# Result rows gathered in two rounds, and the last expert's rows selected in two parts, in a two-layer trunk with top-2 experts

## The chip, the core and the metric

The kernel is one program on 1 core of one Trainium2 chip. It is measured by device microseconds from the launch to the end of the program, median of several runs. TensorE (PE) multiplies, VectorE (DVE) and ScalarE (ACT) move and compute elementwise, GpSimd (POOL) issues the indexed transfers, SyncE (SP) issues the loads of the weights. Each engine runs its own list of instructions in order, and they meet at semaphores only.

## What is computed

A trunk of two layers over 512 tokens of width 1024, float32. Layer 0 mixes with an mLSTM and differential attention, layer 1 with a short gated convolution. Behind either mixer stands the part that the change is about: a router picks for each token one group of four experts and two experts in it, out of sixteen in all, and adds their weighted outputs.

```python
def hier_moe(h, wg, bg, we, be, w_gate, w_up, w_down):
    ...
    _, gsel = lax.top_k(glog, 1)
    ...
    top_v, top_i = lax.top_k(elog_g, EXPERT_TOP_K)
    top_w = jax.nn.softmax(top_v, axis=-1)
    eid = gsel * EXPERTS_PER_GROUP + top_i
    combine = jnp.einsum('tk,tke->te', top_w, jax.nn.one_hot(eid, N_EXPERTS, dtype=jnp.float32)) * pg[:, None]
    ...
    for e in range(N_EXPERTS):
        y = (jax.nn.silu(t @ w_gate[e]) * (t @ w_up[e])) @ w_down[e]
        out = out + combine[:, e:e + 1] * y

def reference(x, ...):
    for layer in range(DEPTH):
        h = rmsnorm(x, norm_mix[layer])
        ...
        x = x + y.astype(x.dtype)
        h = rmsnorm(x, norm_ffn[layer])
        x = x + hier_moe(h, ...).astype(x.dtype)
    return rmsnorm(x, norm_final)
```

## The kernel before

**Weights and precision.** Every large product runs as three fp32r matmuls on a high and a low part of both operands (`mm3`, L1834 to L1838). SP loads the weights into `ring`, six slots of 1 MB, two chunks each; ScalarE writes the high part of a chunk (L672, in layer 1's mixer with a gain, L670), VectorE the low part (L1073, L1070). Both parts lie in `w_split`, which holds six chunks, so ScalarE starts on a chunk when TensorE has finished the one six before it.

**Experts.** An expert has room for 96 tokens (`CAP`). GpSimd gathers the rows of the tokens of the next expert (L617), TensorE turns them (`turn_xg`, L2171). The step of expert e on TensorE is: its gate (4 chunks), the turning of the activations of expert e-1 (L2195), its up projection (4 chunks), the turning of expert e+1's rows, and the down projection of e-1 (4 chunks). In the step of expert 14 the activations of 14 itself are turned midway through the down projection of 13, so that expert 15's step can begin with the down projection of 14. VectorE's part of a step: half of an output row copied (L1633), the low parts of the weights, the low part of the activations (`copy_actT`, L1597), the gated product (`hidden`, L1604), the low part of the next rows (L1590). ScalarE copies the other half and issues the store of the 96 rows to `y_rows_dram` (L955).

**The way back.** `result_rows` (L1542 to L1562) computes on VectorE where in `y_rows_dram` each token's two rows lie, `back_idx`; a token whose row is of expert 15 gets the index of its other row there, since expert 15 is not fetched. When experts 0 to 14 are stored, GpSimd issues eight gathers, for four tiles of 128 tokens two each, into `y_back` (`take_back`, L634). VectorE adds them to the tokens with their weights (`combine`, L1535). The rows of expert 15 come by TensorE: a selection matrix `selT` times `y_sb` as plain fp32 (`last_rows`, L2270), added by `add_last` (L1523). Expert 15's rows are stored all the same (L950). In layer 1 the last tile is summed wholly on TensorE (L2279 to L2281). If an expert has more than 96 tokens, a branch that each engine takes on `overflow_flag` handles the rest; it is not taken here.

After layer 0's experts VectorE combines tiles 0 and 1, adds the last expert's rows, splits the first odd weights, and ScalarE squares and scales the tiles for the next norm (L716, L722), GpSimd computes the roots (L539, L542), TensorE turns them (L1811). After layer 1's experts the same leads to the final norm and the stores of the result. `keep_busy` (L1826) is filler: matmuls whose result nobody reads.

## Time and profile before

| | us |
|---|---|
| median of 3 runs | 1113.03 |
| lowest, highest | 1112.18, 1113.85 |
| span of the profiled execution | 1108.9 |

The span runs from the first to the last instruction of one execution; the difference to the median lies around it. TensorE is busy for 1078.4 us of it, VectorE for 870.7, ScalarE for 662.6, GpSimd for 114.7. A timeline row gives the start, the duration, the engine, the line and the operation; in square brackets the idle time ahead of it and what ended it. A row of the waits gives who waited for whom. "PEld" is the load of a weight into TensorE. In the chain of waits each row is released by the one above it. Windows give the busy time of the engines in a stretch.

### The profile page before, as it was taken

The numbers are of one execution on the slowest core, as the hardware profiler recorded it, in microseconds if no ns is written. First come the engines' busy times: TensorE is split into PE (matmuls) and PEld (weight loads), VectorE is DVE, ScalarE is ACT, GpSimd is POOL, SyncE is SP. The second block draws the span as 40 slices with busy tenths as digits, with TensorE's granted clock in tenths as the row PEclk, the third lists the DMA queues.
The fourth block names the chain that finished last, engine by engine and source line by source line (L and its number), as shares of the span: only waits on it lengthen the run. The fifth ranks groups of instructions, "written<-read, shape, count | busy, mean of one in ns | idle before, by whom it ended". The sixth has DMA issues, their size and how long they took to land.

```text
span 1108.9 us, 15258 instructions
## 1 busy us (share of the span) xinstructions
PE 1078.4 (97%) x5352; PEld 875.6 (79%) x5352; DVE 870.7 (79%) x1139; ACT 662.6 (60%) x848; POOL 114.7 (10%) x160
## 2 busy tenths in 40 slices
PE   7999999999999999999999999999999999999996
PEld 5777777678878888888886888878978888888883
DVE  5256765788799999999999453654699999999997
ACT  5224444523488888878876413222488888778872
POOL 2010000222120000011013000000120000010013
PEclk9999999999999999999999999999999999999998
DMA  9742222112389999999999522332189999999985
GB/s 326 196 149 77 86 86 77 62 72 77 115 304 392 406 396 397 408 393 410 399 386 327 177 79 77 114 100 90 77 305 392 406 396 396 409 395 410 400 338 211
DMA packets 78643, 285.89 MB, mean 258 GB/s; under 512 B 17687, under 2 KB 17687, under 8 KB 62204
## 3 DMA queue, kind: packets, MB, share of 16 engines
q1 hardware_dynamic: 66396, 241.64, 57.0%
q0 software_dynamic: 8464, 30.42, 8.3%
q10 hardware_dynamic: 3728, 13.11, 2.9%
q8 instruction: 33, 0.54, 0.2%
q14 instruction: 22, 0.18, 0.0%
HBM read 266.27 MB, written 20.20 MB: 258 GB/s over the span
## 4 chain that ended last, share of the span: by engine, by line
PE 67%; DMA 15%; DVE 10%; ACT 3%; issue 2%; POOL 2%; POOLq 0%; DVEq 0%; SPq 0%; ACTq 0%
PE ps L1836 20%; PE ps L1838 19%; PE ps L1837 19%; DMA ring<-in_exp_w_gate 10%; DVE w_split L1073 5%; ACT w_split L672 2%; DMA arena<-h_rows_dram,arena 2%; DMA arena<-y_rows_dram,arena 1%; PE ps L2171 1%; DMA y_rows_dram<-arena 1%; PE ps L2085 1%; POOL arena L634 1%; PE ps L2107 1%; PE ps L1811 1%; PE ps L1920 1%
## 5 line engine op out<-in xcount | busy, mean ns | idle before, releaser
L1073 DVE TENSOR_TENSOR w_split<-ring,w_split 128x1024 fp32r<-128x1024 f32 x428 | 505.1, 1218 | 46.8 <-ACT w_split L672 39.1
L672 ACT CAST w_split<-ring 128x1024 fp32r<-128x1024 f32 x428 | 441.8, 1052 | 128.6 <-PE ps L1838 90.2
L1836 PE MATMUL ps<-w_split,hT 128*128 128x512 f32 (+1 forms) x976 | 385.6, 395 | 3.7 <-DVE hT L1581 1.7
L1838 PE MATMUL ps<-w_split,hT 128*128 128x512 f32 (+1 forms) x976 | 377.7, 387 | 0.0
L1837 PE MATMUL ps<-w_split,hT 128*128 128x512 f32 (+1 forms) x976 | 376.8, 386 | 0.0
L1836 PEld LDWEIGHTS ps<-w_split,hT 128*128 128x128 f32 x976 | 183.5, 188 | 43.8 <-issue 2.9
L1838 PEld LDWEIGHTS ps<-w_split,hT 128*128 128x128 f32 x976 | 183.3, 188 | 38.0
L1837 PEld LDWEIGHTS ps<-w_split,hT 128*128 128x128 f32 x976 | 183.7, 188 | 34.1
L1836 PE MATMUL ps<-hT,w_split 128*128 128x512 f32 (+1 forms) x384 | 144.8, 377 | 1.8 <-DVE hT L1109 1.0
L1837 PE MATMUL ps<-hT,w_split 128*128 128x512 f32 (+1 forms) x384 | 142.8, 372 | 0.0
L1838 PE MATMUL ps<-hT,w_split 128*128 128x512 f32 (+1 forms) x384 | 142.8, 372 | 0.0
L1836 PEld LDWEIGHTS ps<-hT,w_split 128*128 128x128 f32 x384 | 72.3, 188 | 20.5 <-issue 6.9
L617 POOL DMA_INDIRECT arena<-h_rows_dram,arena x30 | 40.1, 1337 | 413.1 <-PE ps L2171 394.0
L1838 PEld LDWEIGHTS ps<-hT,w_split 128*128 128x128 f32 x384 | 72.3, 188 | 12.8
L1837 PEld LDWEIGHTS ps<-hT,w_split 128*128 128x128 f32 x384 | 72.4, 188 | 12.1
L670 ACT ACTIVATE w_split<-ring,odd_gain 128x512 fp32r<-128x512 f32 x48 | 31.3, 715 | 46.6 <-PE ps L1838 46.4
L1070 DVE SCALAR_TENSOR_TENSOR w_split<-ring,odd_gain,w_split 128x512 fp32r<-128x512 f32 x48 | 33.0, 746 | 31.1 <-ACT w_split L670 30.8
L539 POOL TENSOR_SCALAR st<-st 128x1 f32<-128x1 f32 (+1 forms) x27 | 10.1, 374 | 342.3 <-ACT arena L716 233.6
L716 ACT ACTIVATE arena<-x_sb 128x1024 f32<-128x1024 f32 x19 | 20.1, 1061 | 38.6 <-DVE x_sb L1371 20.7
L805 ACT ACTIVATE x_sb<-x_sb,st 128x128 f32<-128x128 f32 (+3 forms) x32 | 17.8, 557 | 38.0 <-DVE st L1202 38.0
L1590 DVE TENSOR_TENSOR hT<-ps,hT 128x768 fp32r<-128x768 f32 x30 | 28.4, 948 | 3.1 <-ACT hT L893 3.1
L1197 DVE SCALAR_TENSOR_TENSOR x_sb<-ps,arena 128x256 f32<-128x256 f32 (+3 forms) x16 | 13.1, 821 | 18.9 <-PE ps L1920 18.9
(271 smaller groups left out, 914.0 us busy)
## 6 DMA issues: line engine op xcount, KB each, us to landing
ring<-in_exp_w_gate SPq DMA_DIRECT2D x64, 1024.0 KB, 12.5
ring<-in_exp_w_up SPq DMA_DIRECT2D x64, 1024.0 KB, 12.5
ring<-in_exp_w_down SPq DMA_DIRECT2D x64, 1024.0 KB, 13.2
ring<-in_w_in_even SPq DMA_DIRECT2D x14, 1024.0 KB, 11.4
y_rows_dram<-arena ACTq DMA_DIRECT2D x32, 384.0 KB, 7.0
ring<-in_w_in_odd SPq DMA_DIRECT2D x12, 1024.0 KB, 8.7
ring<-in_w_out_even SPq DMA_DIRECT2D x4, 1024.0 KB, 4.7
h_rows_dram<-arena POOLq DMA_DIRECT2D x8, 512.0 KB, 3.2
```

The costliest lines, as they stand in the source:

```text
L617: g.indirect_dma_start(out=xg[0:CAP, e % 2, :], out_offset=None, in_=h_dram, in_offset=bass.IndirectOffsetOnAxis(ap=slot_tok[0:CAP, e:e + ...
L670: ins = s.activation(hi_of(c)[:, row], raw(c)[:, row], ACT.Copy, scale=scale)
L672: ins = s.copy(hi_of(c), raw(c))
L716: s.activation(junk, x_sb[:, t, :], ACT.Square, accum_out=st[:, t:t + 1]).then_inc(sumsq_ready, 1)
L805: s.activation(e_maps[:, u % 2, m, 0:n], e_maps[:, u % 2, m, 0:n], ACT.Exp, bias=st[:, 16 + c:17 + c], accum_out=st[:, 20 + c:21 + c]).the ...
L1070: ins = v.scalar_tensor_tensor(out=lo_of(c)[:, row], in0=raw(c)[:, row], scalar=scale, in1=hi_of(c)[:, row].bitcast(F32), op0=ALU.mult, op ...
L1073: ins = v.tensor_tensor(lo_of(c), raw(c), hi_of(c).bitcast(F32), ALU.subtract)
L1197: v.scalar_tensor_tensor(out=e_maps[:, u % 2, :, 0:n], in0=src, scalar=64.0 ** -0.5, in1=bc(bias_sb[:, h % 2, T - n:T], 1, P, 2, n), op0=A ...
L1590: v.tensor_tensor(xgT[:, u, 1, :, 0:CAP], ps[:, 5:7, :].rearrange("p b (k c) -> p (b k) c", k=4)[:, :, 0:CAP], xgT[:, u, 0, :, 0:CAP].bitc ...
L1836: mm(out, a[0], b[0], start=start, stop=False)
L1837: mm(out, a[1], b[0], start=False, stop=False)
L1838: return mm(out, a[0], b[1], start=False, stop=stop)
```

## The change

**Two rounds of gathers.** Behind the last gather of tokens GpSimd issues eight gathers that read only the rows of experts 0 to 11 (`EARLY`, 1152 rows): `bounds_check` lets them skip an index beyond. They wait until experts 0 to 11 are stored, until `result_rows` is done and until `sel_last` is turned (its memory is part of `y_back`). When expert 14 is stored and the first round has landed, eight more gathers follow with `late_idx`, in which the indices below 1152 have 3072 added, so that these are skipped. A tile is there when four gathers have landed instead of two.

**`result_rows` and the selection matrix earlier.** For this VectorE runs `result_rows` ahead of the step of expert 14 (before: behind it), with two operations more. TensorE turns `sel_last` ahead of that step too (before: behind the down projection of expert 14), and ScalarE copies it to `selT` there.

**The last expert.** Its output is no longer stored. ScalarE writes the high part from PSUM to `y_last` (in `hT`, where the even experts' rows were), VectorE the low part (`last_low`, two subtractions), and `last_rows` multiplies both parts by `selT` as fp32r, 16 matmuls in layer 0 and 12 in layer 1. In layer 1 ScalarE copies the fp32 rows to `y_sb` as well, for the last tile. Its tile order is 0, 2, 1, and the two matmuls that don't need gathered rows stand ahead of the wait for them. `last_rows` has two filler matmuls instead of four.

**VectorE at the ends.** Of the odd weights, the first two chunks are split ahead of the combines in layer 0. The combines of tiles 0 and 1 stand in the branches, with `last_low` between them. A semaphore is merged with another at the start.

```diff
@@ pool, experts @@
                 pool.wait_ge(xg_turned, E * (l + 1))
+                pool.wait_ge(flag_ready, l + 1)
+                pool.wait_ge(last_sel_turned, l + 1)
+                pool.wait_ge(y_stored[0], stores_before(l, E - E // GROUPS))
+                pool.wait_ge(y_stored[1], stores_before(l, E - E // GROUPS + 1))
+                for t in range(TT):
+                    for k in range(2):
+                        c = 2 * t + k
+                        g.indirect_dma_start(out=y_back[:, t, k, :], out_offset=None, in_=y_dram[0:EARLY, :],
+                                             in_offset=bass.IndirectOffsetOnAxis(ap=back_idx[:, c:c + 1], axis=0),
+                                             bounds_check=EARLY - 1, oob_is_err=False).then_inc(y_back_loaded[t], 16)
...
+                pool.wait_ge(y_stored[0], 16 * (E // 2) * (l + 1))
+                pool.wait_ge(y_stored[1], 16 * (E // 2 - 1) * (l + 1))
+                for t in range(TT):
+                    pool.wait_ge(y_back_loaded[t], 64 * l + 32)
...
                 with pool.Else():
-                    take_back((E - 1) * CAP)
+                    take_back((E - 1) * CAP, late_idx)
@@ act @@
+            def copy_y_parts(l, down_done):
+                act.wait_ge(chunk_done, down_done)
+                for half in range(2):
+                    s.copy(y_last[0:CAP, 0, half * 512:half * 512 + 512], ps[0:CAP, 2 + half, :]).then_inc(y_last_hi, 1)
+                if l:
+                    act.wait_ge(y_stored[1], stores_before(l, E - 1))
+                    for half in range(2):
+                        act.wait_ge((y_half0, y_half1)[half], E * (l + 1))
+                        s.copy(y_sb[0:CAP, 1, half * 512:half * 512 + 512], ps[0:CAP, 2 + half, :]).then_inc(y_last_hi, 1)
...
-                copy_last_y(1, 2, c + 16, 16 * (n // 2))
-                store_y(E - 1, n, 1)
+                copy_y_parts(l, c + 16)
@@ dve @@
-                v.tensor_copy(back_idx, rt[:, 592:600]).then_inc(flag_ready, 1)
+                link(v.tensor_scalar(late_f, rt[:, 592:600], float(EARLY), float(2 * E * CAP), ALU.is_lt, ALU.mult))
+                v.tensor_copy(back_idx, rt[:, 592:600])
+                v.tensor_tensor(late_idx, late_f, rt[:, 592:600], ALU.add).then_inc(flag_ready, 1)
...
                 for e in (E - 3, E - 2):
-                    step(e, n0 + e, e % 2, step_chunk(l, e), None, 16 * ((n0 + e - 2) // 2))
+                    if e == E - 2:
+                        result_rows(l)
+                    step(e, n0 + e, e % 2, step_chunk(l, e), None, stores_before(l, e - 2))
                 n, c = n0 + E - 1, step_chunk(l, E - 1)
-                result_rows(l)
...
+                if l == 0:
+                    splits(c + 18)
...
+                def last_low():
+                    for half, copied in enumerate((y_half0, y_half1)):
+                        cs = slice(half * 512, half * 512 + 512)
+                        dve.wait_ge(y_last_hi, 4 * l + half + 1 - l * 2)
+                        v.tensor_tensor(y_last[0:CAP, 1, cs], ps[0:CAP, 2 + half, :], y_last[0:CAP, 0, cs].bitcast(F32),
+                                        ALU.subtract).then_inc(copied, 1)
...
+                with dve.Else():
+                    if l:
+                        end_weights()
+                    combine(l, 0)
+                    last_low()
+                    combine(l, 1)
@@ pe, last_rows @@
-                keep_busy(4, 0)
+                keep_busy(2, 0)
...
-                for half in range(2):
-                    cs = slice(half * 512, half * 512 + 512)
+                halves = [slice(half * 512, half * 512 + 512) for half in range(2)]
+                for half, cs in enumerate(halves):
                     mm(ps[:, 6 + half, :], end_selT, y_sb[0:CAP, 1, cs], start=True, stop=False)
+                pe.wait_ge(y_back_loaded[TT - 1], 128)
```

The order of VectorE's instructions at the end of layer 0's experts, before. L1633 opens the step of expert 14, L1545 to L1562 are `result_rows`.

```order
L1633 COPY arena<-ps 96x512
L1073 TENSOR_TENSOR w_split<-ring,w_split 128x1024 x4
L1597 TENSOR_TENSOR hT<-ps,hT 128x4x96
L1073 TENSOR_TENSOR w_split<-ring,w_split 128x1024 x4
L1604 TENSOR_TENSOR arena<-arena,ps 96x512
L1590 TENSOR_TENSOR hT<-ps,hT 128x8x96
L1073 TENSOR_TENSOR w_split<-ring,w_split 128x1024 x2
L1597 TENSOR_TENSOR hT<-ps,hT 128x4x96
L1073 TENSOR_TENSOR w_split<-ring,w_split 128x1024 x2
L1545 TENSOR_SCALAR overflow_flag<-arena 128x1
L1546 SCALAR_TENSOR_TENSOR arena<-arena 128x8
```

The same place now; the lines of the split, of L1633 and of L1597 have become L1103, L1665 and L1629, and `result_rows` begins at L1575 (first fence its beginning, second its end).

```order
L1103 TENSOR_TENSOR w_split<-ring,w_split 128x1024 x4
L1575 TENSOR_SCALAR overflow_flag<-arena 128x1
L1576 SCALAR_TENSOR_TENSOR arena<-arena 128x8
L1578 TENSOR_TENSOR arena<-arena,iota_slot 128x64
L1579 TENSOR_TENSOR arena<-arena 128x128
```

```order
L1592 TENSOR_SCALAR arena<-arena 128x8
L1593 CAST arena<-arena 128x8
L1594 TENSOR_TENSOR arena<-arena 128x8
L1665 COPY arena<-ps 96x512
L1103 TENSOR_TENSOR w_split<-ring,w_split 128x1024 x4
L1629 TENSOR_TENSOR hT<-ps,hT 128x4x96
L1103 TENSOR_TENSOR w_split<-ring,w_split 128x1024 x4
```

`result_rows` stood behind the step's last two splits and now stands ahead of its first operation, with L1592 and L1594 added.

VectorE's order behind layer 0's experts before: L1624 is the last operand of expert 15, L1535 the combines, L1523 `add_last`, L1070 the split of odd weights, two instructions a chunk. The first fence is what stands ahead of the branch, the second what stands behind it.

```order
L1073 TENSOR_TENSOR w_split<-ring,w_split 128x1024
L1614 TENSOR_TENSOR arena<-arena,ps 96x256
L1073 TENSOR_TENSOR w_split<-ring,w_split 128x1024
L1624 TENSOR_TENSOR hT<-ps,hT 128x2x96
L1688 TENSOR_LOAD overflow_flag
```

```order
L1535 SCALAR_TENSOR_TENSOR x_sb<-arena,x_sb 128x1024 x4
L1523 SCALAR_TENSOR_TENSOR x_sb<-ps,arena,x_sb 128x1024 x2
L1070 SCALAR_TENSOR_TENSOR w_split<-ring,odd_gain,w_split 128x512 x2
L1523 SCALAR_TENSOR_TENSOR x_sb<-ps,arena,x_sb 128x1024 x2
L1070 SCALAR_TENSOR_TENSOR w_split<-ring,odd_gain,w_split 128x512 x2
```

And now: L1656, L1100, L1565, L1734 (`last_low`) and L1553.

```order
L1646 TENSOR_TENSOR arena<-arena,ps 96x256
L1103 TENSOR_TENSOR w_split<-ring,w_split 128x1024
L1656 TENSOR_TENSOR hT<-ps,hT 128x2x96
L1100 SCALAR_TENSOR_TENSOR w_split<-ring,odd_gain,w_split 128x512 x4
L1739 TENSOR_LOAD overflow_flag
```

```order
L1565 SCALAR_TENSOR_TENSOR x_sb<-arena,x_sb 128x1024 x2
L1734 TENSOR_TENSOR hT<-ps,hT 96x512 x2
L1565 SCALAR_TENSOR_TENSOR x_sb<-arena,x_sb 128x1024 x2
L1777 UNCONDITIONAL_BRANCH
L1553 SCALAR_TENSOR_TENSOR x_sb<-ps,arena,x_sb 128x1024 x4
```

Four instructions of odd splits moved from among the adds to ahead of everything, and two subtractions stand between the combines.

TensorE's end of layer 1, before and now (L2264 and L2318 turn the last tile's selection, L2270 and L2328 select the other tiles, L2279 and L2347 select for the last tile).

```order
L1826 MATMUL ps<-later,ones 128x512 x4
L2264 MATMUL ps<-arena 96x128
L2270 MATMUL ps<-arena,hT 128x512 x6
L2279 MATMUL ps<-arena 128x512
L2280 MATMUL ps<-arena 128x512
L2281 MATMUL ps<-arena 128x512
```

```order
L1884 MATMUL ps<-later,ones 128x512 x2
L2318 MATMUL ps<-arena 96x128
L2328 MATMUL ps<-hT 128x512 x12
L2347 MATMUL ps<-arena 128x512 x2
L2350 MATMUL ps<-arena 128x512
L2351 MATMUL ps<-arena 128x512
```

The selection matmuls are twice as many, of another type, and both that select for the last tile stand ahead of the products with the gathered rows.

## Rows read from the trace of the kernel before

**Rows 1.** The page, parts 1 and 4: busy time; the chain by engine.
```profile
PE 1078.4 (97%) x5352; PEld 875.6 (79%) x5352; DVE 870.7 (79%) x1139; ACT 662.6 (60%) x848; POOL 114.7 (10%) x160
...
PE 67%; DMA 15%; DVE 10%; ACT 3%; issue 2%; POOL 2%; POOLq 0%; DVEq 0%; SPq 0%; ACTq 0%
```

**Rows 2.** Chain of waits, layer 1's tail: start us, us, what.
```profile
1070.03 6.00 DMA y_rows_dram<-arena
...
1076.29 1.17 POOL arena L634
...
1085.45 8.55 DMA arena<-y_rows_dram,arena
...
1095.24 0.86 PE ps L2280 x2
...
1101.63 1.45 POOLq L75
```

**Rows 3.** Windows: us, then busy us per engine, granted clock, DMA share, GB/s.
```profile
544.90:563.80 18.90, 18.84 (x93) 15.27 (x91) 18.90 (x21) 15.83 (x18) 0.00 (x0) 1.00 1.02 416
1044.10:1065.10 21.00, 20.77 (x102) 16.83 (x101) 21.00 (x22) 17.80 (x21) 0.57 (x1) 1.00 1.02 415
```

**Rows 4.** Waits, layer 1 (first two), layer 0: us, times, longest.
```profile
PEld ps L1836 <- DVE hT L1597: 0.7, 1, 0.7
...
PEld ps L2195 <- DVE arena L1604: 0.2, 1, 0.2
...
PEld ps L1836 <- DVE hT L1597: 0.5, 1, 0.5
```

**Rows 5.** VectorE timeline, layer 1: start us, us, engine, line, operation.
```profile
1058.76 0.68 DVE L1604 TENSOR_TENSOR arena<-arena,ps 96x512 f32<-96x512 f32 x1
...
1062.50 0.55 DVE L1597 TENSOR_TENSOR hT<-ps,hT 128x384 fp32r<-128x384 f32 x1
...
1065.23 0.14 DVE L1545 TENSOR_SCALAR overflow_flag<-arena 128x1 int32<-128x1 f32 x1
...
1068.00 0.17 DVE L1562 CAST arena<-arena 128x8 int32<-128x8 f32 x1
1068.08 1.22 DVE L1073 TENSOR_TENSOR w_split<-ring,w_split 128x1024 fp32r<-128x1024 f32 x1
```

**Rows 6.** VectorE timeline, end of layer 0.
```profile
583.79 0.35 DVE L1624 TENSOR_TENSOR hT<-ps,hT 128x192 fp32r<-128x192 f32 x1
584.72 2.60 DVE L1535 SCALAR_TENSOR_TENSOR x_sb<-arena,x_sb 128x1024 f32<-128x1024 f32 x2 [0.58 <-DMA arena<-y_rows_dram,arena]
...
590.85 2.48 DVE L1523 SCALAR_TENSOR_TENSOR x_sb<-ps,arena,x_sb 128x1024 f32<-128x1024 f32 x2
593.24 1.41 DVE L1070 SCALAR_TENSOR_TENSOR w_split<-ring,odd_gain,w_split 128x512 fp32r<-128x512 f32 x2
```

**Rows 7.** ScalarE, then TensorE, end of layer 0.
```profile
583.42 3.79 ACT L670 ACTIVATE w_split<-ring,odd_gain 128x512 fp32r<-128x512 f32 x6
...
596.32 2.14 PE L1811 MATMUL ps<-ident,arena 128*128 128x128 f32 x16 [1.20 <-ACT arena L722]
```

**Rows 8.** VectorE (first two), then ScalarE, end of layer 1.
```profile
1084.26 5.24 DVE L1535 SCALAR_TENSOR_TENSOR x_sb<-arena,x_sb 128x1024 f32<-128x1024 f32 x4
...
1099.57 0.69 DVE L1791 TENSOR_TENSOR x_sb<-ps,x_sb 128x512 f32<-128x512 f32 x1 [1.89 <-PE ps L2281]
...
1086.56 0.58 ACT L919 COPY arena<-ps 96x512 f32<-96x512 f32 x1 [3.81 <-PE ps L1838]
```

**Rows 9.** Windows behind the last matmul, columns as in rows 3.
```profile
1099.60:1103.60 4.00, 0.00 (x0) 0.00 (x0) 3.56 (x4) 0.72 (x2) 1.78 (x2) 0.96 0.32 130
1103.60:1108.00 4.40, 0.00 (x0) 0.00 (x0) 0.92 (x2) 0.00 (x0) 0.00 (x0) 0.50 0.61 239
```

**Rows 10.** Line L634, result gathers: ns min, median, max.
```profile
L634 POOL DMA_INDIRECT arena<-y_rows_dram,arena x16: 937/986/1880, 577.5 to 1085.5; - x16
```

**Rows 11.** Line L315, weight loads of layer 1's last steps.
```profile
DMA to landing us min/median/max: 11.3/12.5/13.6
```

129 lines of the change are left out of this document (76 added, 53 removed).

## The prediction

> **What bounds the kernel now.** I read the page first, then the chain of waits, then the busy windows, then the timelines of the places that the diff touches. TensorE is busy 97% of the span and carries 67% of the chain that ended last [rows 1]: where it runs, the time is TensorE's. The diff touches four short places: the step of expert 14 and the tail after expert 15, in either layer. The question is what ends last there.
>
> At the end of layer 1 the chain of waits says: the store of expert 14's rows starts at 1070.03 and takes 6.00 us, only then GpSimd issues eight gathers, the last is issued at 1085.45 and lands 8.55 us later, and then TensorE sums the last tile [rows 2]. This is the path that the early gathers aim at. But a chain shows one path, not what runs beside it at the same length. So look at VectorE: in 1044.10 to 1065.10 it is busy 21.00 us of 21.00, and in layer 0 18.90 of 18.90; the DMA engines are full there too (415 GB/s) [rows 3]. And TensorE waits in both layers for VectorE's last operation of that stretch, L1597, which makes the activation operand of expert 14: 0.7 and 0.5 us on the weight load, and 0.2 us for L1604 [rows 4]. VectorE, without a gap, already sets TensorE's pace in that step.
>
> **1. The row numbers move ahead of step 14.** `result_rows` ran behind that step. It takes from 1065.23 to 1068.08, 2.85 us [rows 5]; TensorE then had split weights in hand and no wait follows. The change puts it ahead of L1633 of step 14, in the gapless stretch. It gains two operations and a link: the link costs about 0.2 us and the rest 0.1 (L1562 lasts 0.17 us, and the next one starts 0.08 behind it [rows 5]). Sum 3.15 us. Behind it stand 4 splits, L1597, 4 splits, L1604, L1590, 2 splits, L1597. None of them has idle time ahead of it that could swallow the delay, so the first L1604 (1058.76) and the second L1597 (1062.50) come 3.15 us later, and TensorE with them: it waits at the transposes of expert 14's activations and at the down projection. Bounds: 0, if something I don't see lets VectorE catch up; 3.5, if ScalarE, whose store waits for L1633, adds a little. I take **+3.1 us** of TensorE time per layer. Nothing comes back in the step of expert 15: the queue there is free of `result_rows`, but TensorE did not wait for it there. The four selection transposes and ScalarE's copy of them, which move to the same place, take under 0.6 us of ScalarE, which is not full; nothing.
>
> **2. End of layer 0.** VectorE's last operand stands at 584.14 (L1624), it waits 0.58 us for gathered rows, combines tiles 0 and 1 with one more wait, and starts the first `add_last` at 590.85 [rows 6]. From its end hang square, norm, scaling, the transposes at 596.32 (1.20 us of idle TensorE) and all that follows [rows 7]. After the change the same stretch holds, from 587.3 (584.14 + 3.1): two chunks of split odd weights moved ahead of the combines (1.41 us for two halves, so 2.8 [rows 6]), preceded by 0.5 us of wait for ScalarE (its six halves start at 583.42, now 586.5, and the first two end 1.3 us later [rows 7]); combine 0, 2.6 us (L1535 x2 [rows 6]); the low parts of expert 15's rows, two subtractions from PSUM like L1604, which lasts 0.68 us [rows 5], overlapped 1.2; combine 1, 2.6. 587.3 + 0.5 + 2.8 + 2.6 + 1.2 + 2.6 = 597.0, against 590.85: **+6.1 us**. The gathers are no longer awaited: expert 14's store, 3.1 later, lands at about 580.3, and a second-round pair needs some 3 us of issue and under 6 of landing, so tile 0 stands before 590.6. That removes both waits (0.58 and about 0.9), but the moved splits and the new subtractions are longer. Eight plain fp32 selection matmuls become sixteen fp32r ones; TensorE was ahead of VectorE there, so this gives nothing.
>
> **3. End of layer 1.** VectorE combined tiles 0 and 1 in 5.24 us from 1084.26 and had a wait of 1.89 us before the last half of tile 3, at 1099.57 [rows 8]. After: combine 0 ends at 1090.0 (+3.1). The low parts need ScalarE's copies, which can't start before TensorE's last matmul (L919 at 1086.56 [rows 8], now 1089.7), so they run 1090.3 to 1091.5. Then the old sequence, without its 1.89 us of wait: everything behind `add_last` 0 is 4.6 us late (3.1 + 0.3 + 1.2), less about 2.0: VectorE ends tile 3's second half 2.6 us later than before. TensorE is ready by then (1098.4 by the same bookkeeping: end_sel and low parts 1091.5, tile 1 by 1093.1, six fp32 products of 0.87 us as in [rows 2]). Behind it stand ScalarE's square of tile 2 and two halves, now back to back, up to 3.5 us late; GpSimd's last power step took 1.45 us [rows 2] beside a VectorE that was busy, and may be shorter once VectorE is done. Bounds 2.6 and 3.5; I take **+3.0 us**.
>
> **4. The clock.** The last matmul ends at 1099.57, where L1791 starts [rows 8]. TensorE's granted clock is 0.96 in the mean of the 4.0 us behind it and 0.50 after that [rows 9], 1.2 of 2.4 GHz. In layer 0 TensorE, done with the short matmuls at about 597, now waits to 602.4 for the first scaled tile, 5.4 us instead of 1.20 [rows 7]. That is longer than the gap which ended in the fall, so a fall is more likely than not. The transposes there take 2.14 us [rows 7] and would take up to 2.1 more, the nine filler matmuls behind them 1.9. Bounds 0 and 3; I take **+1.5 us**.
>
> **5. The gathers themselves.** A gather costs GpSimd 0.94 to 1.88 us [rows 10]; with the bound a skipped row may cost nothing or as much as a fetched one. Even at the old 8.55 us of landing [rows 2], tile 3 would stand at 1098 and the products at 1101.6, before VectorE asks for them at 1102.2. Nothing either way. The early round starts at about 1057.4, behind the transposes of expert 15's rows.
>
> **Sum.** 6.1 + 3.0 + 1.5 = 10.6 us on the profiled span of 1108.9. The median of the runs is 1113.03, 4.1 us above the span; I add the same difference: 1113.0 + 10.6 = **1123.6 us**. A measurement of this kernel can tell about 0.2%, 2.2 us, from no change.
>
> **Rivals.** (a) *The gather chain was the only thing that ended last.* For it: the chain itself [rows 2]. Then the 1.5 us of waits in layer 0 and the 1.9 in layer 1 go and nothing takes their place: 1113.0 - 3.4 = **1109.6**. It decides if VectorE has 3 us to spare in step 14 and 4 in the tails. Against it: [rows 3] and [rows 6]. 0.08.
> (b) *Step 14 absorbs the row numbers, the tails don't.* Layer 0 then has 6.1 - 3.1 = 3.0, layer 1 3.0 - 3.1, about 0: **1116.0**, or down to 1113.5 if ScalarE's copies come a little early. Against it the gapless stretch. 0.12, a third of it within 0.2% of before.
> (c) *The early gathers hold up the weights.* Twelve of sixteen experts' rows, 3.1 of the 4.2 MB that eight gathers of 128 rows of 4 KB move, now flow while the DMA engines are full with expert 15's weights [rows 3]: 7.6 us of transfer at 415 GB/s. A load takes 12.5 us to land [rows 11], and the split ring lies up to six chunks ahead of TensorE, so I expect most of it hidden. If half comes through, with or without slower gathers (all at 1.88 us, a second round ends 7 us later), both layers lose 2 to 4 us more: about **1129**. 0.17.
> The Trainium skill, "DMA: Bandwidth & Descriptors", section "Queues, rings and completion order", says that each DMA engine takes turns between the queues that have work. By it the weights would keep about half of the bandwidth while the gathers last, and the delay would be nearer to the small end; no run here shows two long queues beside each other. The same notes, "SBUF — State Buffer", say that GpSimd can be locked out by VectorE operations with two SBUF inputs; by that rule the early gathers, issued beside the splits, would be the slow ones. The row has 1.88 at most [rows 10], and the first round has some 20 us.
> (d) *The change does not do what it says:* the bound doesn't save a row's transfer. By part 5 that changes nothing; it belongs to the forecast.
>
> **How the numbers follow.** Forecast 0.63 (1119 to 1127 by its bounds), (a) 0.08, (b) 0.12, (c) 0.17. The predicted time is the forecast's. The range runs from (b) with a small margin to the middle of (c), 1115.5 to 1129.5; it leaves out (a), a part of (b) and the upper half of (c), about 0.2. Faster by over 0.2%: 0.08, rival (a). Within 0.2%: 0.04, of (b). Slower: the rest, 0.88.
>
> **What would show it.** In the profile of the changed kernel: a wait of TensorE for VectorE of 2 to 3 us in step 14 of either layer (right for step 1; none means (a) or (b)); the first `add_last` of layer 0 about 6 us later, with VectorE busy ahead of it and no wait for a gather (step 2); no TensorE wait at the last tile, VectorE without a gap from combine 0 to the end (step 3); a granted clock under 1.00 behind the transposes of layer 1's first norm (step 4; none, and 1.5 us go). ScalarE waiting for loads near the early gathers would be (c). A second-round gather that VectorE waits for would break part 5.

## The result and the profile after

The changed kernel takes 1126.12 us (median of 6 runs, 1122.67 to 1127.55), the kernel before in the same comparison 1112.61 us (6 runs, 1109.52 to 1114.47). The ratio is 1.0121, 95% interval 1.0104 to 1.0138: 13.5 us slower. The prediction was 1123.6 us, range 1115.5 to 1129.5, with 0.88 for slower.

The profiled run of after is 1127.55 us, its span 1125.8, against 1108.9 before: 16.9 us between the two profiles. So the profiles themselves stand 3.4 us further apart than the medians, and a difference between two spans has to be taken apart before it is explained. The page, parts 1, 3 and 4, of after:

```profile
PE 1084.0 (96%) x5348; PEld 882.5 (78%) x5348; DVE 874.1 (78%) x1147; ACT 662.2 (59%) x850; POOL 149.0 (13%) x176
...
q0 software_dynamic: 10768, 30.43, 8.3%
...
PE 77%; DVE 8%; DMA 7%; ACT 3%; issue 3%; POOL 2%; POOLq 0%; DVEq 0%; SPq 0%; ACTq 0%
```

Against [rows 1] the chain has less DMA and more TensorE: the path through expert 14's store and its gathers, which ended last before, is not the one that the chain picks now. In layer 0 it picks the early round instead: its gathers up to the one at 577.19, which lands 5.60 us later, and then the second round up to the wait of VectorE. GpSimd is 34 us busier, with 16 more operations.

**Where the time went.** The clearest measure is the length of the two stretches that the change touches, from the first VectorE operation of step 14 to a fixed mark behind the tail: the first projection matmul of the odd layer for layer 0, the last scaled row for layer 1. VectorE's timeline of after, then two rows of before for the same marks (start us, us, engine, line, operation, idle time ahead and its releaser), then TensorE's first projection of after and of before:

```profile
549.85 0.14 DVE L1575 TENSOR_SCALAR overflow_flag<-arena 128x1 int32<-128x1 f32 x1
...
552.98 0.68 DVE L1665 COPY arena<-ps 96x512 f32<-96x512 f32 x1
...
563.13 0.67 DVE L1636 TENSOR_TENSOR arena<-arena,ps 96x512 f32<-96x512 f32 x1
...
1060.15 0.14 DVE L1575 TENSOR_SCALAR overflow_flag<-arena 128x1 int32<-128x1 f32 x1
...
1118.66 1.41 DVE L1121 SCALAR_TENSOR_TENSOR arena<-x_sb,st,arena 128x512 f32<-128x512 f32 x2 [1.09 <-POOL st L569]
```
```profile
549.39 0.68 DVE L1633 COPY arena<-ps 96x512 f32<-96x512 f32 x1
...
1048.61 0.68 DVE L1633 COPY arena<-ps 96x512 f32<-96x512 f32 x1
...
1103.10 1.42 DVE L1091 SCALAR_TENSOR_TENSOR arena<-x_sb,st,arena 128x512 f32<-128x512 f32 x2 [0.44 <-POOL st L559]
```
```profile
610.19 0.36 PE L1894 MATMUL ps<-hT,w_split 128*128 128x256 f32 x1
```
```profile
600.96 0.35 PE L1836 MATMUL ps<-hT,w_split 128*128 128x256 f32 x1 [0.54 <-issue]
```

Layer 0's stretch: 600.96 - 549.39 = 51.57 us before, 610.19 - 549.85 = 60.34 after, **+8.8**. Layer 1's: 54.49 before, 58.51 after, **+4.0**. Together +12.8 of the 13.5 us. The two spans differ in three more places: 0.5 us ahead of step 14 of layer 0, 2.3 us between the two stretches, and 1.3 us behind the last scaled row. The first two lie where the two programs are alike. Between the stretches the kernels of this document take 446.3 to 452.2 us (before 447.65), and a part of that is the granted clock in layer 1's routing, which moves from run to run; windows of before (first) and after, columns as in rows 3:

```profile
790.00:800.00 10.00, 9.41 (x71) 8.99 (x71) 7.62 (x36) 5.74 (x7) 3.00 (x6) 0.83 0.53 210
800.00:811.00 11.00, 10.14 (x75) 8.98 (x75) 9.70 (x21) 7.12 (x10) 3.86 (x2) 1.00 0.27 89
```
```profile
790.00:800.00 10.00, 10.00 (x59) 8.68 (x58) 4.17 (x22) 3.21 (x4) 0.12 (x1) 0.83 0.01 2
800.00:811.00 11.00, 10.40 (x80) 9.98 (x80) 8.36 (x37) 6.03 (x7) 2.99 (x6) 0.84 0.48 191
```

The 1.3 us at the end are a part of the change; the section on the experiments comes back to them. In what follows every kernel is read by these two stretches; the median of the runs stands beside them.

**Step 14.** Waits of TensorE in after, layer 0 (first) and layer 1 (line waited for: us, times, longest), and windows of layer 0:

```profile
PE ps L2253 <- DVE arena L1636: 1.7, 1, 1.7
...
PE ps L2253 <- DVE arena L1636: 2.1, 1, 2.1
```
```profile
564.00:566.00 2.00, 2.00 (x9) 1.66 (x9) 2.00 (x3) 0.48 (x1) 1.70 (x2) 0.66 1.02 426
566.00:568.00 2.00, 2.00 (x6) 1.51 (x5) 1.51 (x3) 1.04 (x1) 1.82 (x1) 0.50 0.98 391
```

`result_rows` takes 3.13 us (549.85 to 552.98), L1636 comes 3.1 us later behind the start of the stretch, and TensorE waits for it where it did not before ([rows 4] had 0.2 us). In layer 0 the granted clock, at 1.00 up to 564, falls behind that wait to 0.50, 1.2 of 2.4 GHz, for some 3 us. VectorE's last operand of expert 15 (L1656) starts at 588.07, 38.22 us behind the start of the stretch, where [rows 6] gives 583.79 - 549.39 = 34.40: 3.8 us. Layer 1, where the clock stays at 1.00, has 37.23 against 34.40. So 2.8 us are the row numbers and 1.0 is the clock.

**Layer 0's tail.** VectorE, then GpSimd's gathers (L638 the last of the first round, L654 the second round), then TensorE, all of after:

```profile
588.07 0.35 DVE L1656 TENSOR_TENSOR hT<-ps,hT 128x192 fp32r<-128x192 f32 x1
589.08 2.74 DVE L1100 SCALAR_TENSOR_TENSOR w_split<-ring,odd_gain,w_split 128x512 fp32r<-128x512 f32 x4 [0.66 <-ACT w_split L690]
591.74 2.60 DVE L1565 SCALAR_TENSOR_TENSOR x_sb<-arena,x_sb 128x1024 f32<-128x1024 f32 x2
594.37 1.28 DVE L1734 TENSOR_TENSOR hT<-ps,hT 96x512 fp32r<-96x512 f32 x2
596.46 2.60 DVE L1565 SCALAR_TENSOR_TENSOR x_sb<-arena,x_sb 128x1024 f32<-128x1024 f32 x2 [0.80 <-DMA arena<-y_rows_dram,arena]
599.31 4.86 DVE L1553 SCALAR_TENSOR_TENSOR x_sb<-ps,arena,x_sb 128x1024 f32<-128x1024 f32 x4 [0.24 <-PE ps L2328]
```
```profile
560.17 3.95 POOL L638 DMA_INDIRECT arena<-y_rows_dram,arena  x1 [33.98 <-PE ps L2229]
...
577.19 1.80 POOL L638 DMA_INDIRECT arena<-y_rows_dram,arena  x1 [0.30 <-issue]
584.66 0.99 POOL L654 DMA_INDIRECT arena<-y_rows_dram,arena  x1 [5.66 <-issue]
```
```profile
604.11 3.68 PE L1869 MATMUL ps<-ident,arena 128*128 128x128 f32 x16 [3.33 <-ACT arena L742]
```

The first `add_last` comes 49.46 us behind the start of the stretch instead of 41.46, +8.0. VectorE is all but full on the way, yet it waits 0.80 us for a gather: the second round starts at 584.66, where the gathers of before started at 577.47 (first row of L634 in [rows 10]). Both chains, VectorE's work and the gathers, end within a microsecond of each other. This is the sentence on which the experiments hang.

From the first `add_last` to the first projection it is 10.88 us instead of 10.11. The transposes take 3.68 us at half clock where they took 2.14, but they start 4.80 us behind `add_last` instead of 5.47: GpSimd's first two small steps take 0.19 and 0.57 us here, and took 0.63 and 0.96 us before.

**Layer 1's tail.** The last rows of VectorE and two of GpSimd beside them, of after:

```profile
1101.63 1.28 DVE L1734 TENSOR_TENSOR hT<-ps,hT 96x512 fp32r<-96x512 f32 x2 [0.40 <-ACT hT L957]
...
1116.29 1.28 DVE L1121 SCALAR_TENSOR_TENSOR arena<-x_sb,st,arena 128x1024 f32<-128x1024 f32 x1 [0.72 <-POOL st L552]
```
```profile
1114.46 1.17 POOL L549 TENSOR_SCALAR st<-st 128x1 f32<-128x1 f32 x1 [1.56 <-ACT arena L736]
...
1116.34 1.28 POOL L562 TENSOR_SCALAR st<-st 128x1 f32<-128x1 f32 x1
```

There is no wait for the last tile's products any more, VectorE goes through; but its small helper steps on GpSimd, 0.2 us elsewhere, take 1.2 us beside VectorE's work and are waited for.

### The profile page after: what moved, and what is told of

Its sections match the earlier page's. It is cut to its first block, busy times and chain, and to the rows that moved or that the text cites. A ratio compares the mean times of both kernels' runs of the same rounds, so it can differ in the third digit from the quotient of the medians.

```text
span 1125.8 us, 15308 instructions
## 1 busy us (share of the span) xinstructions
PE 1084.0 (96%) x5348; PEld 882.5 (78%) x5348; DVE 874.1 (78%) x1147; ACT 662.2 (59%) x850; POOL 149.0 (13%) x176
## 3 DMA queue, kind: packets, MB, share of 16 engines
q0 software_dynamic: 10768, 30.43, 8.3%
## 4 chain that ended last, share of the span: by engine, by line
PE 77%; DVE 8%; DMA 7%; ACT 3%; issue 3%; POOL 2%; POOLq 0%; DVEq 0%; SPq 0%; ACTq 0%
PE ps L1894 23%; PE ps L1896 22%; PE ps L1895 22%; DMA ring<-in_exp_w_gate 4%; DVE w_split L1103 3%; PE ps L2229 2%; DMA arena<-h_rows_dram,arena 2%; PE ps L1869 1%; ACT w_split L692 1%; DMA arena<-y_rows_dram,arena 1%; DVE x_sb L1565 1%; PE ps L2143 1%; POOL arena L638 1%; PE ps L1978 1%; PE ps L2092 1%
## 5 line engine op out<-in xcount | busy, mean ns | idle before, releaser
L1103 DVE TENSOR_TENSOR w_split<-ring,w_split 128x1024 fp32r<-128x1024 f32 x428 | 505.1, 1219 | 52.8 <-ACT w_split L692 45.8
L1896 PEld LDWEIGHTS ps<-hT,w_split 128*128 128x128 f32 x384 | 72.4, 188 | 12.6
L1100 DVE SCALAR_TENSOR_TENSOR w_split<-ring,odd_gain,w_split 128x512 fp32r<-128x512 f32 x48 | 32.9, 746 | 31.7 <-ACT w_split L690 31.5
L638 POOL DMA_INDIRECT arena<-y_rows_dram,arena x16 | 33.2, 2072 | 73.9 <-PE ps L2229 69.6
```

The source lines that it names most:

```text
L638: g.indirect_dma_start(out=y_back[:, t, k, :], out_offset=None, in_=y_dram[0:EARLY, :], in_offset=bass.IndirectOffsetOnAxis(ap=back_idx[:, ...
L1100: ins = v.scalar_tensor_tensor(out=lo_of(c)[:, row], in0=raw(c)[:, row], scalar=scale, in1=hi_of(c)[:, row].bitcast(F32), op0=ALU.mult, op ...
L1103: ins = v.tensor_tensor(lo_of(c), raw(c), hi_of(c).bitcast(F32), ALU.subtract)
L1896: return mm(out, a[0], b[1], start=False, stop=stop)
```

## Experiments

The table gathers all of them. L0 and L1 are the two stretches described above, "sum" their sum against before's 106.06 us; the ratio is to before on the same chip.

| kernel | L0 | L1 | sum | median us | ratio, 95% |
|---|---|---|---|---|---|
| before | 51.57 | 54.49 | 0 | 1112.61 | |
| after | 60.34 | 58.51 | +12.8 | 1126.12 | 1.0121 (1.0104 to 1.0138) |
| rows_ahead | 55.35 | 57.14 | +6.4 | 1117.92 | 1.0042 (1.0026 to 1.0058) |
| rows_back | 62.51 | 64.09 | +20.5 | 1136.37 | 1.0204 (1.0188 to 1.0221) |
| odd_back | 59.63 | 59.57 | +13.1 | 1128.07 | 1.0146 (1.0129 to 1.0164) |
| fill | 58.84 | 58.50 | +11.3 | 1128.74 | 1.0147 (1.0128 to 1.0166) |
| bound1152 | 63.60 | 61.70 | +19.2 | 1132.95 | 1.0166 (1.0148 to 1.0184) |
| one_round | 59.46 | 58.46 | +11.9 | 1126.51 | 1.0105 (1.0082 to 1.0127) |
| hold_clock | 58.75 | 58.55 | +11.2 | 1125.08 | 1.0098 (1.0078 to 1.0118) |
| gps_after | 56.43 | 55.54 | +5.9 | 1121.31 | 1.0073 (1.0052 to 1.0093) |
| sel_fp32 | 61.04 | 57.64 | +12.6 | 1127.91 | 1.0140 (1.0117 to 1.0164) |
| branch_first | 58.47 | 59.53 | +11.9 | 1127.29 | 1.0140 (1.0118 to 1.0161) |
| gps_before | 52.40 | 53.61 | -0.1 | 1112.48 | 1.0003 (0.9986 to 1.0019) |
| gps_sel_one | 53.88 | 55.11 | +2.9 | 1114.74 | 1.0032 (1.0017 to 1.0047) |

Each stretch is from one profiled execution, so a microsecond between two of them is not much; the medians carry some 2 us of their own. Three things can be told apart:

- **The clock in step 14.** In nine kernels the row numbers stand ahead of step 14 on VectorE, and TensorE waits there for 1.3 to 2.1 us. Behind that wait the granted clock fell to 0.50 in layer 0 of after, rows_ahead, odd_back, one_round, hold_clock and sel_fp32, and in layer 1 of rows_ahead, odd_back and branch_first. There the last operand of expert 15 starts 38.2 to 38.3 us behind the start of the stretch, in the other nine places 37.2 to 37.3. A fall costs 1.0 us, and it came or stayed away in the same code, so two stretches are to be compared with the same number of falls.
- **The end.** Behind the last scaled row the span goes on for 5.8 to 5.9 us in the five kernels without an early round (before, rows_ahead, gps_before, one_round, gps_sel_one) and for 7.1 to 7.2 us in the nine with one. GpSimd's closing drain is what ends last there, 6.24 us in one_round and 7.54 us in after. So the early round costs 1.3 us more that no stretch holds, and the sum for the changed kernel is +14.1 us.
- **Layer 1's tail before.** From the last operand to the last scaled row it takes 20.09 us in the profile of before, and 18.86 in both rows_ahead and gps_before, which have the same code there. So 54.49 may be 1.2 us long, and the cost in layer 1 that much higher.

My theory after the result: VectorE's 3.1 us in step 14 go one to one to TensorE; in the tail VectorE is the bound, and the rest is the clock. The rivals: the tail makes up for step 14; the gathers set the end.

### 1. The row numbers alone (rows_ahead)

The kernel before with

```
                 for e in (E - 3, E - 2):
+                    if e == E - 2:
+                        result_rows(l)
...
                 n, c = n0 + E - 1, step_chunk(l, E - 1)
-                result_rows(l)
```

> The kernel before with one edit: its own row numbers (2.85 us of VectorE) ahead of step 14 in both layers. Theory: plus 2.85 us of TensorE time per layer, plus 0.7 in layer 0 if the clock falls there too: 1112.6 + 6.4 = 1119.0 us. The rival, by which step 14 absorbs them or the tail makes up for them: 1112.6; they then cost less behind the step than they did ahead of it, and the end of layer 1, where VectorE had 1.89 us of wait, could take up to 2 of it: 1117.

Measured: 1.0042, 4.7 to 5.4 us; the stretches +3.8 and +2.65, sum 6.4, the size expected but not made up as expected. The last operand of expert 15 comes 3.9 us later in both layers (38.28 against 34.40), 2.9 by the row numbers and 1.0 by the clock; layer 1's tail is 1.2 us shorter, as it is in gps_before, where nothing stands ahead of step 14. TensorE waits 2.1 us for VectorE's L1604 in either layer, and the clock falls in both; layer 0:

```profile
555.00:575.00 20.00, 17.85 (x80) 14.33 (x80) 17.39 (x18) 15.56 (x19) 0.00 (x0) 0.91 1.01 407
```

The rival by which the tail absorbs it is out: 3.9 us of lateness go in, and in layer 0 3.8 come out. The whole tail behind step 14 simply moves: 45.24 us to the first `add_last` instead of 41.46, both waits for gathers still there.

### 2. The row numbers back, in the changed kernel (rows_back)

The reverse edit, in the changed kernel.

> The changed kernel with the row numbers (result_rows) back behind step 14, both layers; all else as changed. Theory (VectorE has no gap in step 14, so the 3.13 us go one to one to TensorE): TensorE's experts end 3.1 us earlier in each layer, and 0.7 us more in layer 0, where the granted clock fell to 0.50 behind the wait of 1.75 us; the early gathers start some 11 us later and still end before expert 14's rows are stored. 1126.1 - 6.9 = 1119.2 us. The profile should show TensorE's wait for VectorE L1636 in layer 0 back at under 0.7 us and the clock at 1.00 there. Rival (the tail, with the gathers and the low parts, is what costs; step 14's delay would be made up by the end): 1126, no difference. Rival 2: the early gathers, now beside expert 15's first splits, run into expert 14's second round: 1122 or more.

Measured: 1.0204, 10 us slower than the changed kernel where 7 us faster was expected. TensorE has no wait above 0.3 us in step 14 and the clock there is 1.00, as the theory said. But VectorE, in layer 0 (first) and layer 1:

```profile
596.28 2.61 DVE L1565 SCALAR_TENSOR_TENSOR x_sb<-arena,x_sb 128x1024 f32<-128x1024 f32 x2 [6.70 <-DMA arena<-y_rows_dram,arena]
...
1108.50 2.60 DVE L1565 SCALAR_TENSOR_TENSOR x_sb<-arena,x_sb 128x1024 f32<-128x1024 f32 x2 [9.02 <-DMA arena<-y_rows_dram,arena]
```
```profile
572.53 1.16 POOL L638 DMA_INDIRECT arena<-y_rows_dram,arena  x1 [46.31 <-DVE arena L1594]
...
585.62 1.16 POOL L638 DMA_INDIRECT arena<-y_rows_dram,arena  x1 [0.30 <-issue]
589.75 0.98 POOL L654 DMA_INDIRECT arena<-y_rows_dram,arena  x1 [2.97 <-issue]
```

The first round can't start before the row numbers, its eight gathers take 14.3 us of GpSimd (572.53 to 586.8), and the second round stands behind them on the same engine. Expert 14's rows had landed at 579.2 (stored at 573.2, 6.0 to landing): 10.6 us are lost in the queue. So the move of the row numbers is not free to be undone, it is the price of the early round; and the tail, which I had taken for VectorE's alone, has a second chain beside VectorE.

### 3. The odd layer's splits back (odd_back)

```
-                if l == 0:
-                    splits(c + 18)
```

> The changed kernel without the two chunks of odd-layer splits that VectorE does ahead of the combines of layer 0 (they go back between add_last 1 and 2). Theory: the first add_last of layer 0 comes 2.8 us earlier, plus the 0.66 us of wait for ScalarE ahead of the fourth half, less what the second-round gather of tile 1 (landing around 596.3 in the changed kernel's own time) then adds to its wait of 0.80 us. If the gather holds, combine 1 can't start before 596.3 and only add_last's other conditions move: a gain of 0 to 0.3. If the landing of tile 1 isn't fixed to that moment: 3 us. I expect the gather to take most of it: 1125, with a wait of 2 to 3.5 us of VectorE ahead of combine 1. By the prediction's step 2 (gathers not awaited) 1123.3.

Measured: no gain (1.0146; L0 0.7 us shorter, the first `add_last` 1.4 us earlier). VectorE of this kernel:

```profile
591.55 2.61 DVE L1565 SCALAR_TENSOR_TENSOR x_sb<-arena,x_sb 128x1024 f32<-128x1024 f32 x2 [2.52 <-DMA arena<-y_rows_dram,arena]
```

The 3.4 us taken off VectorE (2.74 and 0.66 of waiting) turn into 2.52 us of wait for the gather of tile 0 and 0.22 for tile 1. The wait is ahead of combine 0 and not of combine 1 as I had written; the size is as expected. The moved splits cost next to nothing: they fill a time in which VectorE would wait. Its L1, the same code as in the changed kernel, is 1.1 us longer by a fall of the clock in step 14.

### 4. The clock (fill, hold_clock)

fill:

```
                 rows(2, 0)
+                if l == 0:
+                    keep_busy(6, 6)
                 rows(0, 1)
```

> The changed kernel with six more filler matmuls (0.21 us each at full clock, 1.3 us) in layer 0 between the high products of tiles 0 and 2 and the low product of tile 0, where TensorE waits 1.40 us for VectorE's low parts. Theory (the clock falls because of the waits around 592 to 597, and half clock costs 1 to 1.5 us at the transposes and the products of tiles 1 to 3): the granted clock stays at 1.00 until 600 at least, the transposes of the second norm take 2.2 instead of 3.68 us: 1124.8 us. Rival: the clock falls all the same in the 3.33 us of idle ahead of the transposes, and nothing is won: 1126.1, or 0.3 more for the filler.

Measured: 1.0147. The clock is 1.00 until 600 and falls in the 4.67 us of idle TensorE ahead of the transposes, which take 3.68 us as before the edit. From the first `add_last` to the first projection matmul it is 10.89 us, in the changed kernel 10.88: nothing won there. Its L0 is 1.5 us shorter ahead of that, 1.0 of it because the clock did not fall in step 14. hold_clock adds

```
             last_rows(0)
+            pe.wait_ge(x_ready, TT + 1)
+            keep_busy(13, 0)
```

> The changed kernel with filler matmuls in layer 0's tail: six as in the run fill, and 13 more (2.8 us at full clock) once the first add_last has freed bank 0, until the first transposes of the next norm. In the run fill the clock stayed at 1.00 up to 600, fell then all the same, and nothing was won. Theory (the remaining idle time of 3 us ahead of the transposes is what drops it): clock at 1.00 from 594 to 620, transposes 2.2 instead of 3.68 us, the odd layer's first projection 2 us earlier: 1124 us. Rival (what is lost there is VectorE's and ScalarE's time, the clock costs nothing): 1126 to 1128.

Measured: 1.0098, 1125.08 us. TensorE of this kernel, and the window of the tail:

```profile
603.08 3.00 PE L1884 MATMUL ps<-later,ones 128*128 128x512 f16 x13 [1.36 <-DVE x_sb L1553]
606.54 2.15 PE L1869 MATMUL ps<-ident,arena 128*128 128x128 f32 x16 [0.46 <-ACT arena L742]
```
```profile
598.00:604.00 6.00, 4.22 (x17) 2.62 (x18) 5.68 (x6) 0.94 (x1) 1.47 (x2) 1.00 0.88 337
```

The transposes take 2.15 instead of 3.68 us, and from `add_last` to the first projection it is 9.43 instead of 10.88: **1.45 us** is what the half clock costs there. The medians say the same sign (2.6 us by the ratios), but their intervals overlap, so the size rests on the profiles.

### 5. The bound (bound1152)

While reading the traces I found that the bound is not what the section on the change says. `EARLY` is set to 1152 rows and, 14 lines on, in the same scope, to 12 (`EARLY, GATES, JOBS = 12, 12, 28`, which orders the even layer's projections). The gathers are written later, with 12. The early round of the changed kernel skips all but 12 rows.

```
-        EARLY = (E - E // GROUPS) * CAP
+        EARLY_ROWS = (E - E // GROUPS) * CAP
```

and the same name in the first round and in `late_f`.

> The changed kernel with the bound of the first round really at 1152 rows. In the changed kernel the name EARLY is set twice in one scope: (E - E // GROUPS) * CAP = 1152, and 14 lines later 12 (the constant of the even layer's jobs); when the gathers are written it is 12. So its first round skips all rows but 12 (DMA engines move 0 to 23 GB/s in the stretch in which the kernel with the late row numbers issues its last early gathers), and the second round moves nearly all 4.2 MB. Here the name is made distinct, nothing else. Theory (the number of gathers and the moment of the second round's start rule, not the bytes): the second round's start is held by the landing of the first round, which now carries 3.1 MB and lands later, by 0 to 2 us; its own rows land sooner, by up to 3 us. 1126 us, plus or minus 1. Rival (the bytes of the second round were what cost): VectorE's wait of 0.80 us and TensorE's of 1.90 us go, 1123 to 1124. Rival 2 (the early bytes hold up the weights of expert 15): a wait of ScalarE for loads, 1129.

Measured: 1.0166, 5 us slower than the changed kernel by the ratio and 7 by the median; the stretches +3.3 and +3.2 against it, in layer 0 without the fall of the clock in step 14 that the changed kernel had. Its GpSimd and VectorE in layer 0, and DMA windows:

```profile
579.27 0.99 POOL L638 DMA_INDIRECT arena<-y_rows_dram,arena  x1 [0.30 <-issue]
592.54 1.38 POOL L654 DMA_INDIRECT arena<-y_rows_dram,arena  x1 [12.28 <-issue]
```
```profile
598.12 2.60 DVE L1565 SCALAR_TENSOR_TENSOR x_sb<-arena,x_sb 128x1024 f32<-128x1024 f32 x2 [5.06 <-DMA arena<-y_rows_dram,arena]
```
```profile
588.00:590.00 2.00, 1.90 (x10) 1.43 (x10) 1.66 (x3) 1.26 (x3) 0.00 (x0) 1.00 0.81 307
590.00:592.00 2.00, 2.00 (x11) 1.65 (x9) 1.68 (x3) 1.52 (x4) 0.00 (x0) 1.00 0.23 83
```

The early rows share full DMA engines with the weights and are through only around 590; the second round waits for them until 592.54, and its own few rows help nobody. Counted from the start of the stretch, the second round starts at 40.4 us instead of 34.8: 5.6 us later, where I had allowed 0 to 2. Both rivals fall: the bytes of the second round were not what cost, and ScalarE waits for no load beyond 1.9 us. So the slip with the name made the changed kernel faster than it was meant to be.

### 6. One round, and where the branch stands (one_round, branch_first)

one_round leaves out the first round and gives the second all rows (the counts of `y_back_loaded` are halved with it).

> The changed kernel without its first round: eight gathers with all rows once expert 14 is stored; the row numbers stay ahead of step 14. Theory: the first round, with its bound of 12 rows, brings nothing; in layer 0 it even holds the second one up by 2.9 us (expert 14's rows land at 581.8, the second round starts at 584.66, when the last early gather has landed). Without it combine 1 doesn't wait 0.80 us: 1125 us, and in layer 1 nothing changes (both land at 1091). Rival (skipping pays, or the early start pays): 1128 or more.

Measured: 1.0105, not to be told from the changed kernel; L0 0.9 us shorter, L1 the same, as expected. No wait of VectorE for a gather is left in layer 0. But the second round starts at 585.38, 8.8 us behind the issue of expert 14's store (576.6, 6.8 to landing): 2.0 us behind the landing, where the kernel before has 0.3 (570.8, 6.4, start 577.47). The changed kernel puts GpSimd's waits ahead of its read of the overflow flag and its branch, the kernel before behind them.

branch_first:

```
-                pool.wait_ge(y_stored[0], 16 * (E // 2) * (l + 1))
-                pool.wait_ge(y_stored[1], 16 * (E // 2 - 1) * (l + 1))
-                for t in range(TT):
-                    pool.wait_ge(y_back_loaded[t], 64 * l + 32)
...
                 def take_back(rows, idx):
+                    pool.wait_ge(y_stored[0], 16 * (E // 2) * (l + 1))
+                    pool.wait_ge(y_stored[1], 16 * (E // 2 - 1) * (l + 1))
+                    for t in range(TT):
+                        pool.wait_ge(y_back_loaded[t], 64 * l + 32)
```

> The changed kernel with GpSimd's three waits ahead of the second round (expert 14 stored, the first round landed) moved behind its read of the overflow flag and its branch, where the kernel before has them. In the one-round run expert 14's rows land at 583.7 and 1087.9, and the gathers start only at 585.38 and 1089.4, 1.2 to 1.7 us later; in the kernel before 0.3 us later. Theory: the read and the branch cost that 1.2 us and stand on the gather chain now. The second round starts some 1 us earlier in both layers; in layer 0 VectorE's wait of 0.80 us goes: 1125.3 us, in layer 1 nothing changes since VectorE does not wait there. Rival (the branch's cost is somewhere else, and the early round's landing is the whole of it): the second round starts where it did, 1126.1.

Measured: 1.0140, no gain in the median. Its gathers, layer 0 and layer 1:

```profile
581.69 0.99 POOL L653 DMA_INDIRECT arena<-y_rows_dram,arena  x1 [5.04 <-DMA arena<-y_rows_dram,arena]
...
1089.11 1.71 POOL L653 DMA_INDIRECT arena<-y_rows_dram,arena  x1 [3.27 <-DMA arena<-y_rows_dram,arena]
```

The time from the landing of expert 14's rows to the second round, in both layers: before 0.3 and 0.3 us; changed 3.2 and 3.4; one_round (branch behind, no early round) 2.0 and 1.5; branch_first (early round, branch ahead) 2.3 and 2.3; gps_sel_one below (neither) 0.9 and 0.9. Against the kernels with neither (0.3 to 0.9), the early round adds 1.4 to 2.0 us, the branch 0.6 to 1.7, and both together 2.3 to 3.1. Taking either off leaves the sum 0.9 us shorter (branch_first has one fall of the clock in step 14 like the changed kernel, but in the other layer). one_round also ends 1.3 us sooner behind the last scaled row. Neither gain stands clear of the noise in the ratios: the other chain, VectorE's, is as long.

### 7. The selection (sel_fp32)

```
-                copy_y_parts(l, c + 16)
+                copy_last_y(1, 2, c + 16, stores_before(l, E - 1))
...
-                    last_low()
...
-                rows(0, 0)
-                rows(2, 0)
-                rows(0, 1)
+                rows(0)
```

`rows(t)` is now one product per half, `selT.bitcast(F32)` by `y_sb`.

> The changed kernel with the last expert's rows selected as in the kernel before: one plain fp32 product per half from ScalarE's copy, no low parts on VectorE, no second pair of copies in layer 1 (TensorE 3 products of four passes instead of 6 fp32r ones; the row numbers, both rounds and the missing store as changed). Theory (VectorE sets the end of both layers, and the low parts cost it 1.2 us in each; TensorE is ahead of it either way, and longer products also keep its clock up in layer 0): 1126.1 - 2.4 - 1.5 to 2 for the clock = 1122 us. Rival (TensorE's longer products end last at tile 1 or 3 of the tail, the fp32r parts pay for themselves): 1126 or more. Rival 2 (in layer 0 the second round's gather of tile 1 holds VectorE anyway, it lands at 596.3): 1124, with a wait of VectorE of 2 us ahead of combine 1.

Measured: 1.0140, no gain. VectorE in layer 0, then TensorE:

```profile
593.89 2.60 DVE L1565 SCALAR_TENSOR_TENSOR x_sb<-arena,x_sb 128x1024 f32<-128x1024 f32 x2 [1.98 <-DMA arena<-y_rows_dram,arena]
597.25 2.61 DVE L1565 SCALAR_TENSOR_TENSOR x_sb<-arena,x_sb 128x1024 f32<-128x1024 f32 x2 [0.75 <-DMA arena<-y_rows_dram,arena]
```
```profile
592.36 7.13 PE L2315 MATMUL ps<-arena,hT 96*128 96x512 f32 x16 [0.22 <-ACT arena L939]
604.89 3.68 PE L1859 MATMUL ps<-ident,arena 128*128 128x128 f32 x16 [5.40 <-ACT arena L742]
```

This looks like rival 2 of the expectation: VectorE has 1.28 us less to do, and its waits for the gathers grow from 0.80 to 2.73 us. But it is not a clean test. In this execution expert 14's store took 8.1 us to land instead of 6.1, and the second round started 0.9 us later behind the start of the stretch. L1 is 0.9 us shorter. The longer plain products kept the clock at 1.00 until 602, but TensorE then idles 5.40 us ahead of the transposes and they run at half clock all the same. TensorE's products are done at 599.5, `add_last` starts at 600.10: they were never late.

### 8. The row numbers on GpSimd (gps_after, gps_before)

`result_rows` as 35 small GpSimd operations between the gathers of tokens of experts 4 to 10, and a wait of `result_weights` for them; VectorE has none of it. Step 14 is then without them, and the early round still starts on time: what experiment 2 could not do.

> The changed kernel with the row numbers worked out on GpSimd, in 35 small operations between the gathers of tokens of experts 4 to 10, and none on VectorE; all else as changed, the early round starts at the same moment. The run with the row numbers back behind step 14 was 10 us slower because the early round then started at 572.5, ended at 586.8 and pushed the second one to 589.75; VectorE waited 6.7 us for it in layer 0 and 9.0 in layer 1. This run has neither delay. Theory (VectorE's 3.13 us go one to one to TensorE in step 14): the waits of 1.75 and 2.12 us for L1636 go, clock 1.00 there, 1126.1 - 6.9 = 1119.2 us. Rival (the gathers set the end of both layers anyway and take the gain back): 1123. Rival 2: GpSimd's operations beside VectorE's last 2 to 5 us each and hold up the gathers of tokens: over 1130.

Measured: 1.0073, 4.8 to 5.3 us faster than the changed kernel by median and ratio; the stretches 3.9 and 3.0 us shorter, sum 6.9 as expected (1.0 of it is the fall of the clock that stays away). TensorE has no wait in step 14 of layer 0 and the clock stays up:

```profile
555.00:575.00 20.00, 19.89 (x95) 16.21 (x94) 17.23 (x18) 16.61 (x21) 12.40 (x8) 1.00 1.03 410
```

> The kernel before with its row numbers on GpSimd (33 small operations between the gathers of tokens of experts 4 to 10) instead of VectorE; nothing else. Theory (2.85 us less on VectorE behind step 14, where TensorE did not wait for it; both layer ends wait for gathers, 0.58 and 0.89 us in layer 0): nothing, 1112.6 to 1113.6 us. Rival (VectorE is what bounds the step of expert 15 too): up to 2.8 us per layer faster, 1107.

Measured: 1.0003. In the kernel before the same 2.85 us cost nothing where they stood. Step 1 of the prediction is settled from three sides: ahead of step 14 the row numbers cost 6.4 us (experiment 1), taken from there they give 6.9 back, behind it they are free.

### 9. All costs undone together (gps_sel_one)

gps_after with sel_fp32, one_round and branch_first's order of waits. What is kept of the change: expert 15 is not stored, the odd splits stand ahead of the combines, the selection's transposes come earlier.

> What is left of the change when its costs are undone one by one: the row numbers on GpSimd, one round of gathers with the waits behind the branch, the rows of expert 15 selected in plain fp32; kept are the missing store of expert 15, two chunks of odd splits ahead of the combines, the order of the selections. Theory (the costs add up: 5.3 for the row numbers, as measured on GpSimd, 2 to 4 for the low parts and the clock, 0.8 for the second round): 1126.1 - 8 to 10 = 1116 to 1118 us on the scale of 1112.6 before. If it comes to 1112 to 1114, the costs found are all there were. Rival (something else in the change costs, such as the moved splits or the earlier turn of the selection): 1119 or more.

Measured: 1114.74 us, 1.0032 (by the ratio 1116 on before's scale); stretches +2.3 and +0.6. VectorE in layer 0, its combines now without a wait:

```profile
589.47 5.24 DVE L1611 SCALAR_TENSOR_TENSOR x_sb<-arena,x_sb 128x1024 f32<-128x1024 f32 x4
594.95 4.86 DVE L1599 SCALAR_TENSOR_TENSOR x_sb<-ps,arena,x_sb 128x1024 f32<-128x1024 f32 x4 [0.24 <-DVE x_sb L1611]
```

From gps_after's +5.9 to +2.9. Selection, early round and branch are worth 3 us together in the stretches, and 1.3 us more behind the last scaled row; the ratios give 4.6. Each alone, with the row numbers in place, gave 0.2 to 0.9 in the sum and nothing clear of the noise in the ratio. That is how two chains of one length would behave. The direct evidence for it is experiment 3; the sum of the single gains (2.0) and the joint one (3.0) lie too near for single profiles to show it. The time is at the low end of what adding the costs gave, or 1 us under it. The 2.3 us left in layer 0 are 1.8 at the first `add_last` (43.26 against 41.46), the moved splits less the gather waits that they fill, and the lower clock behind it. No version here beats the kernel before.

## Why the prediction was right, point by point

**The bound.** "VectorE, without a gap, already sets TensorE's pace in that step" held, and it carried half of the result. The reading that found it was [rows 3] beside [rows 4]: a window without a gap and a small wait at the very operation that would be pushed.

**Step 1, +3.1 per layer.** Right: 3.13 us of VectorE, 2.1 us of it as a wait at L1636 in layer 1 and 0.8 in smaller waits behind it; L1's experts end 2.8 us later (the last operand, L1656 of after, starts at 1097.38, 37.23 us behind the start of the stretch; before it was L1624 at 1083.01, 34.40). In layer 0 it is 3.8, with 1.0 for a fall of the clock that the prediction had only in the tail.

**Step 2, +6.1 at the first `add_last` of layer 0.** Measured +8.0. The sum's VectorE terms came out (splits 2.74 for 2.8, wait for ScalarE 0.66 for 0.5, low parts 1.28 for 1.2), and 0.7 more than the forecast's 3.1 came in from step 14. The step that failed is the sentence "The gathers are no longer awaited". It rested on expert 14's rows landing at 580.3 and the second round starting with them. They landed at 581.5, and the round started at 584.66. The early round's last gather landed only at 582.8, and the read of the flag and the branch came behind that; neither was priced in the working. The wait of 0.80 us is the visible part. The larger part is that this chain runs level with VectorE's, so that VectorE's extra work costs less than it seems and taking it off gives nothing (experiment 3).

**Step 3, +3.0 at the end of layer 1.** Measured +4.0: 2.8 from step 14 and 1.2 in the tail. TensorE waited 1.90 us for a gather and was still in time, as forecast. Under-sized were the ends of the chain: VectorE waits 0.40 us for ScalarE's copy and 0.72 and 1.09 us for GpSimd's steps, of which two take 1.17 and 1.28 us. The prediction had expected GpSimd's steps to become shorter; [rows 2] has 1.45 us for one of them.

**Step 4, the clock, +1.5.** Right in size, 1.45 us by hold_clock. In the changed kernel only 0.8 of it shows between `add_last` and the first projection, because GpSimd's small steps were 0.7 us faster there, which the prediction did not have. Its place was only half right: the clock was at half from 596 on, with TensorE's waits for the parts and not only in the gap ahead of the transposes, and fell in step 14 too.

**Step 5, the gathers cost nothing.** Wrong in its ground, and harmless by luck. The bounded gathers took up to 4.70 us each and not 1.88 at most; eight of them take 19 us of GpSimd, which fitted only because the row numbers came early (experiment 2). I read the bound from its first definition and not from the value in force where the gathers are written, so the 3.1 MB of rival (c) never flowed. With them (bound1152) the kernel is at 1.0166, about where rival (c) stood (1129 us; here 1131 by the ratio, 1133 by the median); but by another way than it said, not weights held up by gathers but gathers held up by weights. Rival (d), that the change doesn't do what it says, was what really was there: worth no time against the sum, as written, and 5 us against what the change meant.

The sum was 10.6 us. The stretches give 12.8 and the end 1.3 more, 14.1 in all, where the medians have 13.5. Against the forecast, layer 0 has 0.7 more from step 14, 1.2 more up to the first `add_last` and 0.7 less behind it; layer 1 has 1.0 more; the 1.3 us of the end had no term at all. That the total lies within 3 us of the forecast is in part luck, since errors of both signs are in it, and the early round that was priced is not the one that ran. Rivals (a) and (b) are out by experiments 1 and 8.

**Two behaviours of the chip that the prediction named.** The first gather of the early round ends at 564.1, 0.9 us behind the end of four gapless splits (563.2), and the second at 567.8, 0.9 us behind the end of the next two (566.9); the quickest take 0.99 us in all. The small steps of 1.17 and 1.28 us in layer 1's tail end together with the scaling of a row on VectorE beside them. The Trainium skill, "SBUF — State Buffer", section "SBUF: two separate sides", says that a VectorE operation with two SBUF inputs can lock out a GpSimd operation that reads SBUF until it has ended. The trace agrees with that, but not every gather beside a split was slow: the one at 573.63 took 0.99 us.

In bound1152 the queue of the gathers had 41 to 49% of the engines' time in the three stretches of 5 us from 575 to 590, that of the weights 35 to 52%, and the gathers were through some 10 us behind the last issue. The Trainium skill, "DMA: Bandwidth & Descriptors", section "Queues, rings and completion order", says that engines take turns between queues. The share of about a half that the prediction took from it is what this trace shows.

## What to carry to other kernels

When the chain of waits names one path, look how long the next one is before pricing its removal: here VectorE's work and the gathers ran level in layer 0, and 3.4 us taken off VectorE came back as 2.7 us of waiting for gathers. Work that is moved to let a transfer start early is paid for where it lands: an engine without a gap passes every microsecond on, while an idle engine (GpSimd here) takes the same work for nothing. And before pricing a bound or a size, read the value that is in force at the line that uses it, not the line that defines it. Last, when profiles are compared, find first what differs without the edit: here one fall of the clock, 1.0 us, is as large as most of the effects looked for.

## What the runs showed of the hardware

- A bounded gather whose rows are nearly all skipped costs GpSimd as much as a full one, 0.99 us at the least against 0.94. Such a gather landed 2.3 us behind its start beside free DMA engines (rows_back, 585.62), and 5.1 to 9.6 us behind it beside busy ones (after, layer 0). Gathers of all rows landed in 4.3 to 8.6 us. The queue of the gathers shows 2304 more packets in after at the same 30.4 MB (q0: 10768, before 8464).
- GpSimd's instructions vary with what VectorE does beside them: the same gather 0.99 to 4.74 us, a 128x1 operation 0.19 to 1.39 us, and a 128x8 one in gps_after up to 4.1 us.
- The granted clock of TensorE fell to 0.50 behind a single wait of 1.7 us within an otherwise full stretch in layer 0 (564 to 568), and did not fall behind the wait of 2.1 us at the same place of layer 1. In branch_first it was the other way round: 1.00 in 560 to 570, 0.83 in the mean of 1070 to 1080. Over nine kernels it fell at 9 of 18 such waits, and each fall cost 1.0 us.
- GpSimd's closing drain, the last thing that the other engines meet, took 7.54 us in after and 6.24 us in one_round, which has eight gathers less in each layer.
- Reading a flag and branching between a wait and a gather adds 0.6 to 1.7 us to the path, if the wait stands ahead of the branch.
